# A mixture-of-experts layer whose gathered token rows have two slots instead of four

## What is computed

```python
def hier_moe(x, rg_w, rg_b, re_w, re_b, w_gate, w_up, w_down):
    ...                       # top group of 4, then the two best of its 8 experts
    gates = jnp.einsum('nk,nke->ne', w2, jax.nn.one_hot(expert, N_EXPERTS, ...))
    hg = jnp.einsum('nd,edf->nef', xt, w_gate)
    hu = jnp.einsum('nd,edf->nef', xt, w_up)
    act = jax.nn.silu(hg) * hu * gates[:, :, None]
    out = jnp.einsum('nef,efd->nd', act, w_down)
```

## Time and profile before

| | |
|---|---|
| median of 3 runs | 693.06 us (691.35 to 695.7) |
| the profiled execution, its own time | 691.8 us |
| its span, as the profile counts it | 690.0 us |
| PE busy in the span | 585.3 us (85%) |
| DVE, ACT, POOL busy | 371.3, 203.4, 97.1 us |
| moved by DMA | 116.27 MB, mean 169 GB/s |
| expert blocks | 35 |

### The profile page before, as it was taken

The page is one execution under the profiler, slowest core; times in us unless marked ns, Lnnn a source line. Parts: engine busy times, 40 slices in busy tenths (PEclk is TensorE's granted clock), DMA queues, the critical chain, the costliest instruction groups (busy, mean ns, idle before and its releaser), DMA issues. The chain is left out here.

```text
span 690.0 us, 9547 instructions
## 1 busy us (share of the span) xinstructions
PE 585.3 (85%) x3149; PEld 498.7 (72%) x3149; DVE 371.3 (54%) x668; ACT 203.4 (29%) x349; POOL 97.1 (14%) x150
## 2 busy tenths in 40 slices
PE   3899999994999998999999629999999999998000
PEld 2899999972998896888887417777777787775000
DVE  4929988999993676466566570111111111111497
ACT  6632113220323263211311103333333333332232
POOL 4300002000000000000000211233232333231000
PEclk9999999997999999999999758999999999999555
DMA  9623111120223333100010368998899999892694
GB/s 320 122 93 65 44 32 30 53 60 0 62 79 121 115 108 123 62 30 32 31 61 32 120 228 265 336 327 294 303 340 315 344 326 360 295 334 100 260 352 167
DMA packets 51439, 116.27 MB, mean 169 GB/s; under 512 B 8434, under 2 KB 26743, under 8 KB 50295
## 3 DMA queue, kind: packets, MB, share of 16 engines
q1 hardware_dynamic: 42899, 92.82, 39.8%
q0 software_dynamic: 6656, 17.84, 7.3%
q10 hardware_dynamic: 1828, 4.96, 2.0%
HBM read 99.75 MB, written 20.68 MB: 175 GB/s over the span
## 5 line engine op out<-in xcount | busy, mean ns | idle before, releaser
L1600 PE MATMUL ps<-at_hT,at_ring 128*128 128x384 f32 x936 | 160.3, 330 | 0.0
L1600 PEld LDWEIGHTS ps<-at_hT,at_ring 128*128 128x128 f32 x936 | 155.5, 188 | 1.2 <-issue 1.2
L1833 PE MATMUL ps<-at_wexp,at_hTm 128*128 128x256 f32 x560 | 128.0, 382 | 0.0
L1833 PEld LDWEIGHTS ps<-at_wexp,at_hTm 128*128 128x128 f32 x560 | 104.6, 192 | 13.3 <-issue 0.3
L1756 PE MATMUL ps<-at_hT,at_mring 128*128 128x512 f32 (+1 forms) x432 | 102.3, 392 | 2.4 <-DVE at_mring L1300 1.7
L1756 PEld LDWEIGHTS ps<-at_hT,at_mring 128*128 128x128 f32 (+1 forms) x432 | 77.4, 182 | 21.5 <-issue 2.1
L1479 DVE TENSOR_TENSOR at_actv<-at_sg,ps 128x128 f32<-128x128 f32 x35 | 10.0, 287 | 148.6 <-ACT at_sg L832 148.6
L1148 DVE SCALAR_TENSOR_TENSOR at_mixT<-at_uc,sb_par,at_mixT 128x1024 f32<-128x1024 f32 x60 | 77.4, 1289 | 2.1
L1853 PE MATMUL ps<-at_wexp,at_actT 128*128 128x512 f32 x140 | 65.9, 593 | 0.9 <-ACT at_actT L840 0.9
L1819 PEld LDWEIGHTS ps<-sb_ident,at_xg 128*128 128x128 f32 x280 | 37.4, 193 | 26.2 <-issue 22.5
L543 ACT ACTIVATE at_wk<-at_x 128x1024 f32<-128x1024 f32 (+1 forms) x27 | 28.6, 1058 | 85.0 <-DVE at_x L1353 52.4
(11 more groups left out here) (214 smaller groups left out, 580.3 us busy)
## 6 DMA issues: line engine op xcount, KB each, us to landing
at_wexp<-in_expert_w_gate SPq DMA_DIRECT2D x35, 512.0 KB, 7.4
at_wexp<-in_expert_w_up SPq DMA_DIRECT2D x35, 512.0 KB, 4.5
at_wexp<-in_expert_w_down SPq DMA_DIRECT2D x35, 512.0 KB, 6.0
at_x<-in_x_prompt SPq DMA_DIRECT2D x16, 512.0 KB, 6.1
at_raw<-in_w_in SPq DMA_DIRECT2D x16, 512.0 KB, 4.1
at_opair<-scratch_out SPq DMA_DIRECT2D x8, 1024.0 KB, 11.8
scratch_h<-at_wk SPq DMA_DIRECT2D x8, 512.0 KB, 2.6
out_y_prompt<-at_x ACTq DMA_DIRECT2D x8, 512.0 KB, 3.2
```

The source lines that it names most:

```text
L1600: mm = pe.matmul(ps[:, bank + r, 0:t1 - t0], w[:, wpart, k * P:(k + 1) * P], hT[:, hpart, k, t0:t1], start=(m, wpart, hpart) == (0, 0, 0), ...
L1833: mm = pe.matmul(ps[:, 2 + j % 2, 0:2 * FF].rearrange("p (g f) -> p g f", g=2), hTm[:, j % 2, k, :], w[:, :, k, :], start=k == 0, stop=k = ...
```

## The change

The tile `xg` gets 2 slots of 128 x 1024 instead of 4. The numbers that depend on it follow: POOL's iteration b is now gather(b+1), then scatter(b-1), and the loop begins at b = -1. The wait of each gather is the same expression, `xt_done` at least b. SP waits for the gather of block 1 instead of block 2 before it loads the weights of experts 3 and up. PE's, ACT's and DVE's lists are unchanged but for the slot and semaphore numbers.

```diff
-XG = 4
+XG = 2
...
-            sp.wait_ge(gath[2], 16)
+            sp.wait_ge(gath[1], 16)
...
-                    gather(NE + o, gcol[:, o:o + 1], scol[:, o:o + 1], NE + o - 3)
-
-            for b in range(-3, NE + 1):
-                if b + 3 < NE:
-                    c = (b + 3) * CAPB
-                    gather(b + 3, gidxs[:, c:c + 1], tab[:, c:c + 1], b if b >= 1 else None)
+                    gather(NE + o, gcol[:, o:o + 1], scol[:, o:o + 1], NE + o + 1 - XG)
+
+            for b in range(1 - XG, NE + 1):
+                ahead = b + XG - 1
+                if ahead < NE:
+                    c = ahead * CAPB
+                    gather(ahead, gidxs[:, c:c + 1], tab[:, c:c + 1], b if b >= 1 else None)
                 else:
-                    if b + 3 == NE:
+                    if ahead == NE:
...
-                    gather_over(b + 3 - NE)
+                    gather_over(ahead - NE)
                 if b >= 1:
                     c = (b - 1) * CAPB
                     scatter(b - 1, tab[:, c:c + 1])
...
-                    if o + 4 < OVER:
-                        gather_over(o + 4)
+                    if o + XG < OVER:
+                        gather_over(o + XG)
                     scatter(NE + o, scol[:, o:o + 1])
```

## The result

The changed kernel takes **1054.13 us** (median of 4 runs, 1053.04 to 1055.98) against 692.26 us for the kernel before: a ratio of 1.518 (95% interval 1.513 to 1.523). The forecast was 1056 us. The profiled execution took 1053.04 us, of which the span is 1051.3; 690.0 before.

A forecast was written before the change was run, and what follows sets the result against it. PE was taken to bound the kernel, with DMA close behind. Stalls of 243.0, 15.2 and 30.3 us, clock and restart 76.8, less 1.3 for earlier waits, add 364.0 to 691.8: 1056 us, range 985 to 1130.

The forecast's parts named there:

- What bounds it: Expert loop before the change: PE sets the pace at 6.2 us per step, DMA share 0.96, POOL two thirds free.
- The slot's semaphore doesn't bind: Wait of gather(m) for T(m-2): claimed not to bind; POOL's order does, as the scatter ahead waits for D.
- the last rival: Not slower: gathers issued once their slot is free, landings up to some 10 us hidden, 692 us; chance 0.02.
- 32 stalls, gathers 0 to 2 ahead of them: Gathers 3 to 34 stand behind scatters 0 to 31 and each stall PE; gathers 0 to 2 do not.
- Hand-over 3.76 + 0.14 us: Each regular stall without its landing: 3.76 us from end of D to gather issue, 0.14 from landing to first transpose.
- Landing 5.1 us: Gather's issue to landing for blocks 3 to 29, while weights load: 5.1 us, from a bracket of 3.7 to 6.5.
- The base of 3.7 us: Median landing of the first four gathers with little else under way; used for blocks 30 to 34.
- the three further blocks: Last three stalls, where POOL also copies the table's column: 6.4 us plus a 3.7 us landing each, 30.3 together.
- Clock and restart 2.4 us per stall: After each stall PE runs 4.35 us at half clock, losing 2.15 us, plus a slower first transpose; 76.8 us over 32.
- The named signs: In the profile after: repeating chain, PE gaps about 9 us, landings 3.7 to 6.5, DMA share near 0.4, mixed clock.
- landing as without load: Rival: gathers land in 3.7 us throughout, 38 us less, 1018 us; chance 0.13.
- the clock that stays up: Rival: PE keeps full clock through the stalls, 69 us less, 987 us; chance 0.07.

The follow-up runs named there:

- first pair of experiments: Against the changed kernel: two slots with POOL's list in the order of before, 691.96 us; four slots with the order of the change, 1056.91 us.

## Why the prediction was right

- **What bounds it** (PE, with the DMA close behind) held, and so did the step that everything hangs on: nothing is left on PE between D(m-3) and the wait for gather(m). The first pair of experiments shows that the order alone does it.
- **The slot's semaphore doesn't bind**: shown by the same pair. The prediction's reason has a slip: T(m-1) is the one that is over a GU and a D earlier. T(m-2), which the gather waits for, is over a whole step before that, as the 11.5 us of the last rival say.
- **32 stalls, gathers 0 to 2 ahead of them**: so counted. Gather 2 landed after 8.8 us, at 422.11, since the weights of expert 3 now start sooner, and T(2) waited 1.64 us for it. The forecast kept up to 1.6 us for this in the range. It cost nothing net, because the loop began 1.5 us sooner (see the last section); that was not foreseen. The row of T(2):

```profile
422.25 1.13 PE L1820 MATMUL ps<-sb_ident,at_xg 128*128 128x128 f32 x8 [1.64 <-DMA at_xg<-scratch_h,at_gidxs]
```

- **Hand-over 3.76 + 0.14 us**: 3.9 and 3.7 us from D to the gather in the two steps shown, 3.72 on average for blocks 3 to 31; the earlier trace rows carried over unchanged.
- **Landing 5.1 us**: 5.26 for blocks 3 to 29. The reasoning (some 1.5 us of weight traffic left when the gather is issued) is borne out by the run with the weights moved. The base of 3.7 us was partly luck. It came from four gathers of 76, 38, 59 and 38 rows, and the prediction didn't ask how many rows the others have; blocks 3 to 29 have 66 on average (11 to 128), which lands about as fast. Where the rows are far from that, the term is off: 4.2 and 4.0 us for blocks 30 and 31 (128 and 74 rows), and 2.6 to 2.8 for the three further blocks (6, 7 and 7 rows), so that term was 4 us too large.
- **Clock and restart 2.4 us per stall**: 2.35 on average, 1.6 to 3.1 in single steps. PE ran at half clock for 4.4 us of each step on average, where the one case in the kernel before had 4.35. That one sample lay so near the average of 32 is luck in part.
- **The named signs**: the chain repeats as described; the gaps are 7.4 to 10.8 us, but 8.6 to 9.0 for the last three where about 10 was said; the DMA share is 0.33 to 0.35 where 0.4 was said. The gathers' line is still L1008, not L1009; lines move only further down.
- **Rivals**: landing as without load fell (5.2 median), the clock that stays up fell as well (mean 0.69 in the window shown), and both were reached only by making them true: 1021 us and 996 us, where 1018 and 987 had been worked out.

## What to carry to other kernels

How many slots a prefetch has and how early its refill is issued are two things. The lead is set by what stands ahead of the refill in its engine's list and by what that instruction waits for; count from there to the first use. The number of slots matters only if a slot comes free later than that, which no run here had. Where the refill stands behind the last work before its use, the whole chain is paid in each step (362 us here); one block earlier a part of it is (83 us). A matrix engine that stood still long enough to lose its clock pays again when it comes back (2.1 us here, after stalls of 7.4 to 10.8 us).

## What the runs showed of the hardware

The clock after short stalls. With a stall of 1.7 us or less (four slots, one block later) PE stayed at full clock, at 2.6 us and more it did not. With 12 filling matmuls, of the steps in which PE stood still for 1.9 to 2.6 us three kept the clock and eight lost it. With 16 it stood still for up to 1.8 us and always kept it. In the changed kernel the fall comes while PE stands still and the rise while GU runs. Windows of 1 us around the stall shown above:

```profile
502.00:503.00 1.00, 0.00 (x0) 0.00 (x0) 0.00 (x0) 0.00 (x0) 0.53 (x1) 1.00 0.67 205
503.00:504.00 1.00, 0.00 (x0) 0.00 (x0) 0.00 (x0) 0.00 (x0) 0.39 (x1) 0.67 1.04 406
504.00:505.00 1.00, 0.00 (x0) 0.00 (x0) 0.00 (x0) 0.00 (x0) 0.12 (x1) 0.50 0.97 336
...
507.00:508.00 1.00, 0.00 (x0) 0.00 (x0) 0.00 (x0) 0.00 (x0) 0.00 (x0) 0.50 0.73 287
508.00:509.00 1.00, 0.30 (x2) 0.34 (x3) 0.00 (x0) 0.00 (x0) 0.00 (x0) 0.50 0.00 0
...
512.00:513.00 1.00, 1.00 (x4) 0.81 (x3) 0.00 (x0) 0.00 (x0) 0.00 (x0) 0.50 0.00 0
513.00:514.00 1.00, 1.00 (x4) 0.81 (x4) 0.00 (x0) 0.00 (x0) 0.00 (x0) 0.71 0.00 0
```

It fell at about 503.3, 2.4 us after D, and rose at about 513.6, 4.9 us after T began. The same windows show the DMA filled from 502.3 to 507.7 with the weights, the scatter and, from 504.88 on, the gather.

A memset on POOL and an instruction on DVE. The clearing of the slots fell from 3.52 us to 1.81, and one small DVE instruction that used to run beside it fell from 1.43 to 0.23 us. Its line before and after:

```profile
L1368 DVE TENSOR_SCALAR sb_goh<-sb_io,sb_gidx x9: 221/230/1425, 289.5 to 397.7; 128x4 f32<-128x4 f32 x8, 64x4 f32<-64x4 f32 x1
```

```profile
L1369 DVE TENSOR_SCALAR sb_goh<-sb_io,sb_gidx x9: 221/230/231, 289.4 to 396.4; 128x4 f32<-128x4 f32 x8, 64x4 f32<-64x4 f32 x1
```

The index table was ready 1.3 us sooner. In the kernel before, the long instance ran from 389.69 to 391.12 and the memset ended at 391.09; after the change it ended at 389.29, before the instruction began. The other profiles bear this out, whatever the order of the gathers: in all five with four slots this instance took 1.43 us and ended 0.02 us after the memset, and in all seven with two slots no instance took more than 0.23 us. One of them, four slots in the new order (memset from 386.41 to 389.93):

```profile
388.52 1.43 DVE L1371 TENSOR_SCALAR sb_goh<-sb_io,sb_gidx 128x4 f32<-128x4 f32 x1
```

So it goes with the size of the memset. Why this instruction is held and the five just before it, which also run beside the memset, are not, no run here shows.
